# Transposed inverse of DeltaNet chunks updated in pairs of chunks, with a stationary matrix put together by VectorE

## What is computed

```python
a_mat = jnp.where(strict, jnp.einsum('bhnid,bhnjd->bhnij', kbeta, kc) * decay, 0.0)
t_mat = lax.linalg.triangular_solve(a_mat + eye, jnp.broadcast_to(eye, a_mat.shape),
                                    left_side=True, lower=True)
u = jnp.einsum('bhnij,bhnje->bhnie', t_mat, vc * bc[..., None])
```

## Time and profile before

| | |
|---|---|
| median of 3 runs | 1253.79 us (1251.59 to 1254.14) |
| profiled execution | 1254.01 us |
| its span, first to last instruction | 1252.1 us |
| TensorE clock granted, mean | 0.992 of full speed |
| busy: TensorE, its weight loads | 1215.2 us, 1132.5 us |
| busy: VectorE, ScalarE, GpSimd | 803.7 us, 514.1 us, 301.8 us |
| chain that ended last, by engine | PE 81%, DVE 9%, issue 4%, ACT 4%, DMA 2% |
| line 805 (updates of b_T), share of that chain | 3% |

### The profile page before, as it was taken

One profiled execution on the slowest core, in us unless ns is written; L12 is line 12 of the kernel. 1 busy time (PEld: TensorE's weight loads), 2 busy tenths in 40 slices (PEclk: granted clock), 3 DMA queues, 4 the chain that ended last, 5 costly groups with the idle time before them and its releaser, 6 DMA issues.

```text
span 1252.1 us, 25551 instructions
## 1 busy us (share of the span) xinstructions
PE 1215.2 (97%) x8814; PEld 1132.5 (90%) x8814; DVE 803.7 (64%) x1958; ACT 514.1 (41%) x1365; POOL 301.8 (24%) x275
## 2 busy tenths in 40 slices
PE   4999999999999999999999999999999998999997
PEld 4999999999999899989998999899999998999996
DVE  6476477656765676577657756775677575565544
ACT  6443334533453445344533543354345445322210
POOL 1114121411232123212321231123213221222211
PEclk9999999999999999999999999999999998999998
DMA  7232453244325432543154325432544274322253
GB/s 240 89 102 59 141 162 102 62 139 161 102 62 156 151 102 62 159 142 109 53 174 134 106 57 180 129 101 56 188 119 127 72 235 125 107 67 90 79 202 137
DMA packets 79646, 151.56 MB, mean 121 GB/s; under 512 B 12353, under 2 KB 22242, under 8 KB 77986
## 3 DMA queue, kind: packets, MB, share of 16 engines
q1 hardware_dynamic: 78542, 149.31, 38.5%
q10 hardware_dynamic: 1024, 1.07, 0.4%
HBM read 132.20 MB, written 17.27 MB: 119 GB/s over the span
## 4 chain that ended last, share of the span: by engine, by line
PE 81%; DVE 9%; issue 4%; ACT 4%; DMA 2%; SPq 1%; DVEq 0%; ACTq 0%
PE PJ L602 17%; PE PJ L598 11%; PE PJ L599 10%; PE PJ L600 10%; PE PJ L603 8%; PE MX L805 3%; PE MX L786 2%; DVE memx L1545 1%; PE MX L797 1%; PE MX L729 1%; PE MX L709 1%; PE PJ L918 1%; PE MD L857 1%; PE MD L896 1%; PE PJ L919 1%
## 5 line engine op out<-in xcount | busy, mean ns | idle before, releaser
L602 PE MATMUL PJ<-h,w_hi 128*128 128x512 f32 x1110 | 416.9, 412 | 0.2 <-DVE memx L1381 0.2
L1915 POOL TENSOR_TENSOR w_lo<-w_raw,w_hi 128x512 fp32r<-128x512 f32 x160 | 215.6, 1348 | 829.9 <-ACT w_hi L990 829.9
L598 PE MATMUL PJ<-h,w_hi 128*128 128x264 f32 (+1 forms) x1248 | 365.9, 293 | 1.2 <-ACT memx L1020 1.2
L599 PE MATMUL PJ<-h,w_hi 128*128 128x264 f32 (+1 forms) x1248 | 353.8, 283 | 0.0
L600 PE MATMUL PJ<-h,w_lo 128*128 128x264 f32 (+1 forms) x1248 | 353.5, 283 | 0.0
L603 PE MATMUL PJ<-h,w_lo 128*128 128x256 f32 x1110 | 310.7, 280 | 0.0
L602 PEld LDWEIGHTS PJ<-h,w_hi 128*128 128x128 f32 x1110 | 208.9, 188 | 43.8 <-DVE w_lo L1350 1.7
L990 ACT ACTIVATE w_hi<-w_raw 128x512 fp32r<-128x512 f32 x320 | 196.7, 624 | 108.2 <-PE PJ L600 76.5
L598 PEld LDWEIGHTS PJ<-h,w_hi 128*128 128x128 f32 x1248 | 235.3, 189 | 5.4 <-issue 3.9
L599 PEld LDWEIGHTS PJ<-h,w_hi 128*128 128x128 f32 x1248 | 235.6, 189 | 1.6
L600 PEld LDWEIGHTS PJ<-h,w_lo 128*128 128x128 f32 x1248 | 234.3, 188 | 0.0
(11 more groups left out here) (325 smaller groups left out, 1826.0 us busy)
## 6 DMA issues: line engine op xcount, KB each, us to landing
w_raw<-in_w_in SPq DMA_DIRECT2D x256, 256.0 KB, 2.7
w_raw<-in_w_out SPq DMA_DIRECT2D x64, 256.0 KB, 2.8
kv<-in_cache_win_k SPq DMA_DIRECT2D x24, 512.0 KB, 4.7
kv<-in_cache_win_v SPq DMA_DIRECT2D x16, 512.0 KB, 4.2
out<-memx SPq DMA_DIRECT2D x16, 260.0 KB, 3.8
mem<-in_x_prompt SPq DMA_DIRECT2D x4, 1024.0 KB, 10.1
S<-in_state_delta SPq DMA_DIRECT2D x8, 512.0 KB, 3.4
out<-S SPq DMA_DIRECT2D x8, 512.0 KB, 2.9
```

What stands on the lines that cost most here:

```text
L598: pe.matmul(ps, wh, h_hi[:, k, tok], start=k == 0, stop=False)
L599: pe.matmul(ps, wh, h_lo[:, k, tok], start=False, stop=False)
L602: pe.matmul(both, wh, h2[:, :, k, tok], start=k == 0, stop=False)
L1915: pool.tensor_tensor(w_lo[:, par, 4 * q:4 * q + 4, :], w_raw[:, q, :, :], w_hi[:, par, 4 * q:4 * q + 4, :].bitcast(F32), ALU.subtract).the ...
```

## The change

For levels 1 to 5 the updates of `b_T` are made in pairs as well: `b_W[:, j]` takes the odd blocks' rows of `b_U`'s chunk j and the even blocks' rows of chunk 2 + j, and one matmul with it as stationary matrix and all 128 columns of Y gives the update of both chunks. VectorE puts `b_W` together by two operations over 128x256 with a column of 0 and 1 for each row: once ahead of level 1 and once behind the updates of each of levels 1 to 4. The columns come as a further constant, `c_odd`, by a DMA on SP's queue. TensorE waits for `mix_W` ahead of these matmuls. The last level stays as it was.

```diff
+    odd = (i[:, None] >> np.arange(LEVELS)[None, :]) % 2
+    t["c_odd"] = np.concatenate([odd, 1 - odd], 1).astype(f)
...
+        b_W = sb("b_W", [P, 2, P])
+        odd_rows = sb("odd_rows", [P, 2, LEVELS])
...
             sp.dma_start(terms[:], c_terms).then_inc(s["s_loaded"], 16)
+            sp.dma_start(odd_rows[:].rearrange("p a n -> p (a n)"), c_odd).then_inc(s["s_loaded"], 16)
...
                     last.then_inc(s["mix_Z"], 1)
-                    for c in chunks if n < LEVELS - 1 else (2, 3):
-                        last = pe.matmul(blocks(mx(3)[:, c, :], n, c // 2), b_U[:, c, :],
-                                         blocks(b_Y[:, c % 2, :], n, c // 2), start=True, stop=True)
+                    if n < LEVELS - 1:
+                        pe.wait_ge(s["mix_W"], (LEVELS - 2) * h + n)
+                        for j in range(2):
+                            last = pe.matmul(crossed(mx(3), n, False, j), b_W[:, j, :],
+                                             b_Y[:, j, :].rearrange("p (k a s) -> p a k s", a=2, s=1 << n),
+                                             start=True, stop=True)
+                    else:
+                        for c in (2, 3):
+                            last = pe.matmul(blocks(mx(3)[:, c, :], n, 1), b_U[:, c, :],
+                                             blocks(b_Y[:, c % 2, :], n, 1), start=True, stop=True)
                     last.then_inc(s["mix_Z"], 1)
...
+            def both_rows(n):
+
+
+                link(dve.tensor_scalar(b_W[:], b_U[:, 2:4, :], odd_rows[:, 1, n:n + 1], None, ALU.mult))
+                dve.scalar_tensor_tensor(b_W[:], b_U[:, 0:2, :], odd_rows[:, 0, n:n + 1], b_W[:], ALU.mult,
+                                         ALU.add).then_inc(s["mix_W"], 1)
+
...
                     dve.tensor_tensor(t, t, all_blocks(mx(0)[:, 2:4, :], 0, odd), ALU.subtract).then_inc(
                         s["mix_T"], 1)
+                dve.wait_ge(s["mix_U0"], 3 * h + 3)
+                both_rows(1)
                 yield from idle(2)
...
                     dve.tensor_tensor(t, t, tz, ALU.subtract).then_inc(s["mix_UT"], 1)
+                    if n < LEVELS - 2:
+                        dve.wait_ge(s["mix_UT"], UTS * h + 2 * n - 1)
+                        both_rows(n + 1)
...
-            dve.wait_ge(s["s_loaded"], 48)
+            dve.wait_ge(s["s_loaded"], 64)
...
-                ch.at(h, 1, 62)
+                ch.at(h, 1, 67)
```

More of the change, by code:

```diff
@@ L175, in build @@
 def build(nc, x_prompt, x_sample, cache_k, cache_v, state_conv, state_delta, g_pre, w_in, w_ba, conv_w, a_log, dt_bias,
-          onorm_w, w_out, g_post, c_ident, c_upper, c_causal, c_levels, c_lnmask, c_rope, c_terms,
+          onorm_w, w_out, g_post, c_ident, c_upper, c_causal, c_levels, c_lnmask, c_rope, c_terms, c_odd,
           y_p, y_s, k_new, v_new, c_new, c_old, st_p, st_s):
@@ L335, in build @@
             "hg_ok mix_T1 mix_ss mix_lnrk mix_rs mix_scal mix_gb mix_tok mix_kbT_ps mix_kbT mix_arg mix_D "
-            "mix_kk mix_qk mix_A mix_QK mix_B mix_U0 mix_T_ps mix_T mix_Y_ps mix_Y mix_Z mix_UT ch_kS ch_r "
+            "mix_kk mix_qk mix_A mix_QK mix_B mix_U0 mix_T_ps mix_T mix_Y_ps mix_Y mix_Z mix_W mix_UT ch_kS ch_r "
             "ch_v_ps ch_v ch_S_ps ch_o_ps ch_S ch_o1 ch_o o_sq on_rs o_n o_T z_sig_b z_ok_b gated_b gB_out S_out "
@@ L2020 @@
         "conv_w", "a_log", "dt_bias", "onorm_w", "w_out", "g_post"]
-_CONST = ["c_ident", "c_upper", "c_causal", "c_levels", "c_lnmask", "c_rope", "c_terms"]
+_CONST = ["c_ident", "c_upper", "c_causal", "c_levels", "c_lnmask", "c_rope", "c_terms", "c_odd"]
 _OUTS = [(1, TP, D), (NB, 1, D), (NH, HD, TT), (NH, HD, TT), (NH, 3, HD, CW - 1 + NB), (NB, CW - 2, CONV_CH),
```

## The result

| | median us | runs | ratio to before, 95% interval |
|---|---|---|---|
| before | 1252.69 | 4 | |
| after | 1274.30 | 4 (1272.87 to 1278.53) | 1.0175 [1.0152, 1.0198] |

What follows compares the result with a forecast made beforehand. TensorE, full inside the head loop, was taken as the bound. Passes -18.0, places A +16.8, B +9.6 and C +3.5 summed to +11.9 us: 1265.9, or 1265.7 us against the median, range 1247.5 to 1273.

Steps and rivals of the forecast that it cites:

- place A: First pair, ahead of VectorE's line 1665: TensorE's line 841 loses 2.25 us in seven heads, 1.05 in the first; +16.8 us.
- 0.45 us of one level: Matmul block of levels 1 to 5: eight passes replace twelve, 1.02 us for 1.47, saving 0.45 us 40 times.
- TensorE's passes: Updates of b_T at levels 1 to 5: four passes fewer per level, -18.0 us in the whole kernel.
- place B: Behind the second pair: VectorE's d_vec chain falls into GpSimd's work, line 863 stalls 1.2 us a head; +9.6 us.
- place C: Behind the fifth pair: d_add comes late for line 875, stalling 0.5 us in seven heads; +3.5 us.
- Rival (1): VectorE gets the turn before GpSimd at A, and B's chain ends before GpSimd comes: faster, 1248.1 us, chance 0.15.
- I take the middle, 1.2: At B, the stall per head chosen between 0.85 us (last operation caught) and 1.55 us (last two caught).
- upper bound of 1.55: At B, both last operations of the chain caught by GpSimd, d_vec at 359.45: a stall of 1.55 us a head.
- the positions, 357.50 against 357.64: At B, GpSimd's line 1915 was to start at 357.50, the chain's last two operations at 357.64 and 357.84.
- upper bound of 0.75: At C, the largest stall of line 875 allowed per head, 0.75 us; the lower bound was 0.
- (5): Rival for the whole kernel: all of VectorE's added work is hidden, -18.0 us, 1235.8 us, chance 0.03.

Runs made afterwards that it cites:

- first experiment: Kernel before with TensorE's part alone, two 128-column matmuls for four at levels 1 to 5, b_U standing in for b_W: 1237.14 us, ratio 0.9878.
- second experiment: Kernel before with only both_rows(1), the first pair of VectorE operations, added between lines 1612 and 1665, nobody reading b_W: 1275.86 us, ratio 1.0175.

## Why the prediction was wrong in size

Two steps failed. The sum had no term for TensorE's clock, which cost 6 us behind the waits at place A; and it took the 0.45 us of one level for all 40, which gave 18.0 us where 15 were measured. Three us and six are nearly all of the miss.

| term | forecast us | found us | from |
|---|---|---|---|
| TensorE's passes | -18.0 | -15 | first experiment |
| place A | +16.8 | +15.8 | 17.2 less the 1.4 of before |
| place B | +9.6 | +10.4 | line 875's wait |
| place C | +3.5 | +4.4 | line 887's wait |
| clock behind A | none | +6 | four heads by 1.5 |
| sum | +11.9 | +21.6 | measured +21.6 |

That the sum meets the measurement to the tenth is chance: the first term alone is uncertain by over 2 us, and with the 16.5 us that the blocks in its trace give, the sum would be 20.1.

The mechanisms that the prediction named were the right ones, one by one:

- **Place A** was right to the order of the queues. Line 1665 was to end at 348.3 against 346.05, 2.25 us late; it was 2.13. In head 0 the wait is 0.80 us, not 1.05. Rival (1), VectorE gets the turn, is out: in all eight heads line 1689 takes 1.75 us or more.
- **Place B**: the step "I take the middle, 1.2" was mis-sized a little. Both operations are caught in every head, which was the upper bound of 1.55; it shows as 1.3 us of wait a head. A range of two cases has no middle that can occur; the positions, 357.50 against 357.64, spoke for the upper one.
- **Place C** came to 0.63 us a head, between the 0.5 and the upper bound of 0.75. GpSimd's turn was there before and after, in another place: line 1478 had taken 1.39 us, and now the fifth pair's first operation takes 1.19 in place of 0.35, while line 1478's successor has its plain length:

```profile
377.18 1.19 DVE L1588 TENSOR_SCALAR b_W<-mem,odd_rows 128x256 f32<-128x256 f32 x1
378.40 0.48 DVE L1589 SCALAR_TENSOR_TENSOR b_W<-mem,odd_rows,b_W 128x256 f32<-128x256 f32 x1
378.80 0.68 DVE L1490 TENSOR_TENSOR memx<-memx,memr 32x520 f32<-32x520 f32 x1
```

  From the start of this stretch to the end of d_add it is 4.67 us, 3.76 before: 0.91 us more, where the sum had 0.8.
- **TensorE's passes**: "0.45 us goes at a level" was read at level 1 and holds at levels 1 and 3. At the other three it is 0.39 (first experiment), and the whole gain is 15 us in place of 18. The step that failed is the multiplication by 40 of what one level's rows show. It explains half of the 3 us; the other half is within what the run can tell.
- **The clock** is the term that the sum did not have. It asked for the length of each wait and not for what a wait of over 2 us does to TensorE behind it. The earlier trace rows show a clock of 1.00 in one head of the loop, and I carried that over to a loop with long waits in it.

The passes' 3 us, B and C's 1.7 and the clock's 6, less 1.0 at A, make the 9.7 us between forecast and result. Without the clock the result would have been some 1268, inside the range. (A slip in the chances, without weight: (1) and (5) make 0.18 for faster, not 0.17, and leave 0.10 for the same.)

What stays open: why the low clock stands behind four of seven waits of the same length. The waits differ by less than 0.1 us, and in the second experiment it was the same four heads. Nothing was run on it.

## What to carry to other kernels

Extra work on an engine with a third of its time free is not free: ask for each insertion what stands behind it in that queue, and whether the fullest engine already waits for that. The same pair cost 23.7 us at one place and nothing one step earlier. Count turns with GpSimd: in these rows, where a VectorE operation on SBUF ends, a GpSimd operation that already waits goes ahead of the next one, for the whole length of its instruction, even if there is no gap between VectorE's two (line 1689 followed the pair at once). The cure here was to hold GpSimd's work back to a place where nobody waits. And where a wait of the matmul engine gets long, add the slow passes behind it, or fill it.

## What the runs showed of the hardware

- TensorE: a float32 pass of 64 columns costs as much as one of 128 in this stream (twelve passes 1.47 us, eight 1.03 or 1.02).
- VectorE and GpSimd: an operation of 8 columns took 1.12 us in place of 0.17 while GpSimd worked on SBUF. A GpSimd operation waiting since 350.66 went ahead of a VectorE operation that came at 350.90. The subtractions from b_T and b_U, with one operand in PSUM, kept their 0.41 us, one of them (376.85) in the midst of a GpSimd mask (376.54, 0.67 us).
- TensorE's clock: of seven idle stretches of 2.3 us in the head loop, four were followed by a clock of 0.50. In three it was low at the first pass, in head 1 it fell just behind the first passes; behind the other three it stayed at 1.00. With idle stretches of 1.5 us or less in the head loop it stayed at 1.00 in all traces. After one of 1.73 us near the end of the kernel it fell to 0.50 within 1.5 us in seven of the nine traces.
